# Transposing normed tiles by DMA instead of by TensorE in a macaron decoder layer

## The chip, the cores and the metric

The kernel runs on the 8 cores of one Trainium2 chip. Every core does the same program on its own prompt of 2048 tokens and its own 16 running sequences of 8 new tokens (128 tokens); nothing is exchanged between cores. The metric is the device time in microseconds of the slowest core.

## The reference

One layer: a half feed-forward, a token mixer, a second half feed-forward, and a last norm. A norm stands before each of the three parts.

```
def rmsnorm(x, g):
    inv = rsqrt(mean(x * x, axis=-1) + EPS)
    return x * inv * g

x = x + 0.5 * (silu(h @ w_gate) * (h @ w_up)) @ w_down      # h = rmsnorm(x, norm_ffn1)
B, C, u, p = split(rmsnorm(x, norm_mix) @ w_in)
y_conv = B * dwconv3_causal(C * u)
y_pool = (trailing means over 2/4/8/16 of p, minus p) @ pool_w * pool_scale
x = x + concat(y_conv, y_pool) @ w_out
x = x + 0.5 * SwiGLU_2(rmsnorm(x, norm_ffn2))
y = rmsnorm(x, norm_final)
```

D_MODEL is 1024, D_FF 2816. The states of the convolution and of the pooling are outputs too. Weights and activations come in float32; the matmuls run in bfloat16.

## The kernel before

**Data.** The 2176 tokens of a core are 17 tiles of 128. `xres` holds all of them in SBUF in float32, tokens on partitions. `hT` holds the normed tokens in bfloat16 with the features on partitions (8 blocks of 128 features), the form in which the matmuls of the gate, up and `w_in` projections take them. Between the two a tile must be transposed.

**The norm of a tile** has four steps: nA1 (ScalarE: square and row sum, line 357), nA2 (GpSimd: two tiny operations, lines 363 and 365), nA3 (VectorE: scale by the row's factor and by the weight `gbc`, into one of four bfloat16 buffers `hp`, line 370) and norm_B. norm_B is the transpose: eight TensorE transposes of 128x128 into one PSUM bank (line 387) and one ScalarE copy of the bank into `hT` (line 391). `norm_seq` lays the steps of a group of four tiles in a row: four nA1, four nA2, four nA3, four norm_B.

**The feed-forwards** (`run_ffn`) go over 6 blocks of 3 or 4 times 128 columns of D_FF, and in each over 5 groups of tokens: four of 512 tokens (four tiles) and one of 128 (tile 16). A pair (block, group) is an item. An item emits its gate and up products GU (line 454, 16 matmuls for each 128 columns; then Silu on ScalarE, line 460, and the product on VectorE, line 462), interleaved with the down products D of the item before (line 484, two for each tile, each added to `xres` on VectorE, line 491). In block 0 the norm steps of group g+1 are merged among the D of item (0, g), so the first GU of item (0, g+1) needs tiles whose norms end in item (0, g). In the last block of the first feed-forward the norms for the mixer are merged in the same way, one item later, and are read only in the mixer.

**The mixer** goes over 8 groups of 256 prompt tokens and one of 128 (lines 526, 548, 682, 704). The norms of the last five tiles for it are set into its first two groups by `LATE_SCHED`; the norms of tiles 0 to 3 for the second feed-forward are put into groups 2 to 7 by `trickle`; those of tiles 4 to 7 begin in group 8, and their norm_B stand in item (0, 0) of the second feed-forward.

**Queues.** The order on every engine is the order in which the program emits operations. Loads of weights (float32 in DRAM to bfloat16 in the six `ring` slots) are issued from GpSimd; loads of tokens, of `gbc` and the outputs are issued from SP. The loads of tokens 8 to 16 wait for the first block of down weights. The weights of block 1 are issued when the last TensorE operation of item (0, 0) is done.

Of the kernel before, what the change touches and what calls it, by code (L numbers as in the profile page):

```python
# [132 lines left out]
def build_nc():  # L133
# [216 lines left out]
    def hpbuf(k):  # L350
        return hp[:, k, :] if k < 3 else hp3[:, :]
# [22 lines left out]
    tb_cnt = [0]  # L374
    tb_banks = [[7, 6]]

    def norm_B(tt, bank=None):
        k = hp_of[tt]
        if bank is None:
            bank = tb_banks[0][tb_cnt[0] % len(tb_banks[0])]  # L380
            tb_cnt[0] += 1
        pst = ps[bank][:, :].bitcast(BF16)

        def pe_fn(e):
            ins = None
            for kc in range(KC):
                ins = e.transpose(out=pst[:, kc * 128:(kc + 1) * 128], in_=hpbuf(k)[:, kc * 128:(kc + 1) * 128],  # L387
                                  identity=idb[:, :])
            return ins
        P.op("pe", pe_fn, reads=[("hp", k), ("idb",)], writes=[("ps", bank)])  # L390
        P.op("act", lambda e: e.activation(out=hT[:, :, tt * 128:(tt + 1) * 128],  # L391
                                           in_=pst.rearrange("p (a b) -> p a b", a=KC), func=AF.Copy),
             reads=[("ps", bank)], writes=[("hT", tt)])
# [538 lines left out]
            emit()  # L932
        return []

    norm_tiles(FG[0][2])
    load_first_block(2, len(BLOCKS[0]), False)

    def after_lead1():
# [20 lines left out]
    def ffn1_post(g):  # L959
        if not state.get("gbc_mix"):  # L960
# [2 lines left out]
        return norm_seq(FG[g][2])  # L963

    late_norm = run_ffn(1, pre1, ffn1_post, ffn1_block_start, tail_fn=lambda: load_mix_units(["p", "o0"]),
                        defer_tail=True, lead=12, after_lead=after_lead1)

    def ffn2_slots(b):
        return (3, 0, 1) if b % 2 == 0 else (2, 4, 5)
# [5 lines left out]
    def mixer_phase2_setup():  # L975
# [6 lines left out]
    assert len(late_norm) == 4 * len(LT) and len(LT) == 5  # L982
    LATE_SCHED = {
        0: [(nA1, LT[0]), (nA2, LT[0]), (nA1, LT[1]), (nA2, LT[1])],
        1: [(nA1, LT[2]), (nA2, LT[2]), (nA3, LT[0])],
        2: [(nA1, LT[3]), (nA2, LT[3]), (nA3, LT[1]), (norm_B, LT[0])],
        3: [(nA3, LT[2]), (norm_B, LT[1])],
        4: [(nA1, LT[4]), (nA2, LT[4]), (nA3, LT[3]), (norm_B, LT[2])],
        5: [(nA3, LT[4]), (norm_B, LT[3])],
        6: [(norm_B, LT[4])],  # L990
    }
    trickle = {}
    for t in range(4):
        trickle.setdefault((t + 2, 1), []).append(lambda t=t: nA1(t))
        trickle.setdefault((t + 2, 2), []).append(lambda t=t: nA2(t))
        trickle.setdefault((t + 3, 1), []).append(lambda t=t: nA3(t))
        trickle.setdefault((t + 4, 1), []).append(lambda t=t: norm_B(t))
    tb_banks[0] = [5, 6]
    for g in range(9):
        if g == 2:  # L1000
# [70 lines left out]
    for g in range(1, len(FG)):  # L1071
        pre2[(0, g - 1)] = norm_seq(FG[g][2])
    so_stage, so_fin = sample_state_out_seq()
    pre2[(0, 0)] = so_stage + [lambda t=t, i=i: norm_B(t, bank=4 + i % 2) for i, t in enumerate(FG[1][2])] + so_fin
    run_ffn(2, pre2, ffn2_post, ffn2_block_start, post_now=True, last_order=[4, 0, 1, 2, 3])

    fin = P.op("sp", lambda e: None)
# [68 lines left out]
```

How the kernel before makes its waits and increments, by code:

```python
    def emit_engine(self, e, eng):  # L121
        waited = {}
        for o in self.byeng[e]:
            ws = [(d.sem, d.val) for d in o.waits] + o.extra_waits
            for (s, v) in ws:
                if waited.get(s, 0) < v:
                    eng.wait_ge(s, v)
                    waited[s] = v
            ins = o.fn(eng)
            if o.sig and ins is not None:
                ins.then_inc(o.sem, 16 if o.dma else 1)
```

## Time and profile before

| | |
|---|---|
| median of 3 runs | 1284.82 us (1284.4 to 1289.32) |
| span of the profiled execution, slowest core (core 7) | 1284.4 us, the same as the fastest of the three times |
| spans of the 8 cores | 1266.5 to 1284.4 us |
| TensorE (PE) busy | 1198.6 us, 93% |
| VectorE (DVE) busy | 596.5 us, 46% |
| ScalarE (ACT) busy | 322.9 us, 25% |
| GpSimd (POOL) busy | 162.6 us, 13% |
| packets of the DMA queues | 21.4% of 16 engines for GpSimd's queue, 5.0% for SP's |

The page follows one execution on its slowest core. "Idle before" is the time in which an engine did nothing ahead of an instruction, with what released it; idle time of an engine that is not the bottleneck costs nothing.

### The profile page before, as it was taken

Reading aid. Unit: us, or ns where it says so; the run is one execution under the profiler, and the core shown is the slowest. Engines: PE = TensorE matmul, PEld = TensorE weight load, DVE = VectorE, ACT = ScalarE, POOL = GpSimd, SP = SyncE. Lnnn points to the kernel's source line nnn. Section 1 sums busy time; section 2 is a strip of 40 time slices with the busy share of each in tenths; the row PEclk is TensorE's granted clock in tenths of the full one; section 3 lists DMA queues with packets and bytes.
Section 4 is the critical chain, followed back from the end, with each engine's and each line's share of the span. In section 5 each row is a group of like instructions: output and inputs, shape, how many; then the busy total and the mean of one; then the engine's idle time right before and its main releaser. Section 6 shows DMA issues by size and latency. Waiting matters only on the chain.

```text
span 1284.4 us, 19776 instructions; the slowest of 8 cores (1266.5 to 1284.4 us)
## 1 busy us (share of the span) xinstructions
PE 1198.6 (93%) x6916; PEld 626.8 (49%) x6916; DVE 596.5 (46%) x933; ACT 322.9 (25%) x714; POOL 162.6 (13%) x283
## 2 busy tenths in 40 slices
PE   3869999999999999979999979999999999999994
PEld 1434544445445444567676744454454454444541
DVE  2345434334334354665555552643443343444567
ACT  3342111111111112664354444421111111111133
POOL 4210000000000001233324240000000000000022
PEclk9889999999999999999999999999999999999998
DMA  9870600600403114050000057016014031040024
GB/s 174 152 185 6 98 13 1 99 1 4 71 1 47 29 29 71 1 102 18 1 2 2 1 86 131 1 17 98 2 26 74 1 51 25 1 74 1 11 105 164
DMA packets 51281, 63.37 MB, mean 49 GB/s; under 512 B 12479, under 2 KB 39103, under 8 KB 51184
## 3 DMA queue, kind: packets, MB, share of 16 engines
q0 software_dynamic: 42768, 41.03, 21.4%
q1 hardware_dynamic: 8416, 21.08, 5.0%
q8 instruction: 57, 0.93, 0.3%
q14 instruction: 40, 0.33, 0.1%
HBM read 93.63 MB, written 9.50 MB: 80 GB/s over the span
## 4 chain that ended last, share of the span: by engine, by line
PE 83%; DMA 6%; DVE 4%; ACT 3%; issue 3%; POOL 1%; SPq 0%; DVEq 0%; ACTq 0%; POOLq 0%
PE ps L454 48%; PE ps L484 24%; PE ps L526 6%; DMA ring<-ffn_up 3%; PE ps L548 2%; DMA xres<-xp 2%; PE ps L704 2%; ACT hT L391 1%; PE ps L387 1%; DMA ring<-ffn_down 1%; DVE tbuf L660 1%; ACT hp L357 1%; DVE xres L491 1%; DVE hp L370 0%; DVE hT L844 0%
## 5 line engine op out<-in xcount | busy, mean ns | idle before, releaser
L454 PE MATMUL ps<-hT,ring 128*128 128x512 bf16 (+1 forms) x3520 | 685.7, 349 | 11.4 <-ACT hT L391 7.8
L454 PEld LDWEIGHTS ps<-hT,ring 128*128 128x128 bf16 x3520 | 319.2, 98 | 355.8 <-issue 20.0
L484 PE MATMUL ps<-ring,scr 128*128 128x512 bf16 x1496 | 359.4, 380 | 15.6 <-DVE xres L491 15.6
L462 DVE TENSOR_TENSOR scr<-scr,ps 128x512 bf16<-128x512 f32 (+1 forms) x220 | 133.5, 607 | 506.9 <-PE ps L454 443.2
L460 ACT ACTIVATE scr<-ps 128x512 f32<-128x512 f32 (+1 forms) x220 | 117.0, 533 | 755.5 <-PE ps L454 749.1
L491 DVE SCALAR_TENSOR_TENSOR xres<-ps,xres 128x512 f32<-128x512 f32 x408 | 275.9, 689 | 52.3 <-PE ps L484 45.7
L484 PEld LDWEIGHTS ps<-ring,scr 128*128 128x128 bf16 x1496 | 143.4, 98 | 180.4 <-issue 23.0
L526 PE MATMUL ps<-hT,ring 128*128 128x256 bf16 (+1 forms) x864 | 95.9, 269 | 4.4 <-ACT scr L649 3.1
L526 PEld LDWEIGHTS ps<-hT,ring 128*128 128x128 bf16 x864 | 80.4, 99 | 15.9 <-issue 5.9
L357 ACT ACTIVATE hp<-xres 128x1024 bf16<-128x1024 f32 x68 | 71.1, 1050 | 43.0 <-DMA xres<-xp 34.0
L370 DVE SCALAR_TENSOR_TENSOR hp<-xres,stt,gbc 128x1024 bf16<-128x1024 f32 x51 | 64.7, 1285 | 24.2 <-POOL stt L365 23.2
L252 POOL DMA_DIRECT2D ring<-ffn_gate x11 | 10.0, 911 | 500.9 <-PE ps L454 491.4
L704 PE MATMUL ps<-ring,scr 128*128 128x512 bf16 x272 | 61.3, 379 | 5.9 <-DVE xres L711 4.9
L387 PE MATMUL ps<-idb,hp 128*128 128x128 bf16 x408 | 33.7, 231 | 33.4 <-DVE hp L370 29.1
L363 POOL TENSOR_TENSOR stt<-stt,deps_t 128x1 f32<-128x1 f32 x68 | 19.6, 289 | 342.5 <-ACT hp L357 311.4
L391 ACT ACTIVATE hT<-ps 128x1024 bf16<-128x1024 bf16 x51 | 51.2, 1021 | 31.7 <-PE ps L387 31.3
L387 PEld LDWEIGHTS ps<-idb,hp 128*128 128x128 bf16 x408 | 27.5, 103 | 45.8 <-issue 40.6
L704 PEld LDWEIGHTS ps<-ring,scr 128*128 128x128 bf16 x272 | 26.0, 98 | 37.8 <-issue 9.3
L365 POOL TENSOR_TENSOR stt<-stt,nhalf 128x1 f32<-128x1 f32 x68 | 41.0, 603 | 10.1 <-POOL stt L363 0.4
L711 DVE TENSOR_TENSOR xres<-ps,xres 128x512 f32<-128x512 f32 x34 | 22.7, 685 | 22.1 <-PE ps L704 22.1
L548 PE MATMUL ps<-hT,ring 128*128 128x256 bf16 (+1 forms) x288 | 31.2, 267 | 0.8 <-ACT scr L687 0.8
L548 PEld LDWEIGHTS ps<-hT,ring 128*128 128x128 bf16 x288 | 26.8, 98 | 3.9 <-issue 1.0
(86 smaller groups left out, 335.5 us busy)
## 6 DMA issues: line engine op xcount, KB each, us to landing
xres<-xp SPq DMA_DIRECT2D x16, 512.0 KB, 13.0
ring<-ffn_down POOLq DMA_DIRECT2D x8, 1024.0 KB, 10.0
ring<-ffn_gate POOLq DMA_DIRECT2D x7, 1024.0 KB, 10.0
ring<-ffn_up POOLq DMA_DIRECT2D x7, 1024.0 KB, 14.3
ring<-w_in POOLq DMA_DIRECT2D x4, 1024.0 KB, 10.4
yp<-hT SPq DMA_DIRECT2D x8, 512.0 KB, 2.7
ring<-ffn_gate POOLq DMA_DIRECT2D x4, 768.0 KB, 8.4
ring<-ffn_up POOLq DMA_DIRECT2D x4, 768.0 KB, 11.6
```

The source lines that it names most:

```text
L357: P.op("act", lambda e: e.activation(out=hpbuf(k), in_=xres[:, tt, :], func=AF.Square, accum_out=stat(k, 0)), reads=[("x", tt, 0), ("x", t ...
L370: P.op("dve", lambda e: e.scalar_tensor_tensor(out=hpbuf(k), in0=xres[:, tt, :], scalar=stat(k, 2), in1=gbc[:, :], op0=ALU.mult, op1=ALU.m ...
L387: ins = e.transpose(out=pst[:, kc * 128:(kc + 1) * 128], in_=hpbuf(k)[:, kc * 128:(kc + 1) * 128], identity=idb[:, :])
L391: P.op("act", lambda e: e.activation(out=hT[:, :, tt * 128:(tt + 1) * 128], in_=pst.rearrange("p (a b) -> p a b", a=KC), func=AF.Copy), re ...
L454: ins = e.matmul(ps[bank][:, 0:N], lhsT=ring_gu(slot)[:, kc, jj * 128:(jj + 1) * 128], rhs=hT[:, kc, tok0:tok0 + N], start=(kc == 0), stop ...
L460: P.op("act", lambda e: e.activation(out=sg[:, sk, 0:N], in_=ps[gb][:, 0:N], func=AF.Silu), reads=[("ps", gb)], writes=[("sg", sk)])
L462: P.op("dve", lambda e: e.tensor_tensor(out=aT[:, buf, jj, 0:N], in0=sg[:, sk, 0:N], in1=ps[ub][:, 0:N], op=ALU.mult), reads=[("sg", sk), ...
L484: ins = e.matmul(ps[db][:, 0:512], lhsT=aT[:, buf, jj, ti * 128:(ti + 1) * 128], rhs=ring_dn(ds)[:, jj, dh * 512:(dh + 1) * 512], start=(j ...
L491: P.op("dve", lambda e: e.scalar_tensor_tensor(out=xs_, in0=ps[db][:, 0:512], scalar=0.5, in1=xs_, op0=ALU.mult, op1=ALU.add), reads=[("ps ...
L526: ins = e.matmul(psh(h)[:, 0:N], lhsT=ring_gu(slot)[:, kc, col * 128:(col + 1) * 128], rhs=hT[:, kc, tok0:tok0 + N], start=(kc == 0), stop ...
L548: ins = e.matmul(ps[bank][:, (gi % 2) * 256:(gi % 2) * 256 + N], lhsT=ring_gu(slot)[:, kc, gi * 128:(gi + 1) * 128], rhs=hT[:, kc, G["tok0 ...
L704: ins = e.matmul(ps[ob][:, 0:512], lhsT=mixT[:, mb, c, ti * 128:(ti + 1) * 128], rhs=ring_dn(slot)[:, c % 4, dh * 512:(dh + 1) * 512], sta ...
```

## The change

norm_B becomes one DMA transpose, issued from SP: it reads the tile in `hp` and writes its place in `hT`. The program gives it blocks of 16 rows by 128 columns, so a tile is 64 of them. Only the first four tiles of the first feed-forward still go through TensorE, by `norm_B_pe`. 47 of 51 tiles change. The transposes that were set apart from their nA3 in the mixer follow it more closely, those of tiles 4 to 7 for the second feed-forward now stand in the mixer's last group, and all four of tiles 4 to 7 of the first feed-forward are emitted ahead of the first GU (`lead` 16 and not 12).

```diff
-    def norm_B(tt, bank=None):
+    def norm_B(tt):
         k = hp_of[tt]
-        if bank is None:
-            bank = tb_banks[0][tb_cnt[0] % len(tb_banks[0])]
-            tb_cnt[0] += 1
+        P.op("sp", lambda e: e.dma_start_transpose(out=hT[:, :, tt * 128:(tt + 1) * 128], in_=hpbuf(k)),
+             reads=[("hp", k)], writes=[("hT", tt)], dma=True)
+
+    def norm_B_pe(tt):
+        k = hp_of[tt]
+        bank = tb_banks[0][tb_cnt[0] % len(tb_banks[0])]
+        tb_cnt[0] += 1
         pst = ps[bank][:, :].bitcast(BF16)
...
-    norm_tiles(FG[0][2])
+    for c_ in norm_seq(FG[0][2], last=norm_B_pe):
+        c_()
...
-                        defer_tail=True, lead=12, after_lead=after_lead1)
+                        defer_tail=True, lead=16, after_lead=after_lead1)
...
-        3: [(nA3, LT[2]), (norm_B, LT[1])],
+        3: [(nA3, LT[2]), (norm_B, LT[2])],
...
-        trickle.setdefault((t + 4, 1), []).append(lambda t=t: norm_B(t))
+        trickle.setdefault((t + 3, 2), []).append(lambda t=t: norm_B(t))
...
             for t_ in FG[1][2]:
                 nA3(t_)
+                norm_B(t_)
             mix_wout(8)
...
-    pre2[(0, 0)] = so_stage + [lambda t=t, i=i: norm_B(t, bank=4 + i % 2) for i, t in enumerate(FG[1][2])] + so_fin
+    pre2[(0, 0)] = so_stage + so_fin
```

On SP's queue, at the start of the kernel, the difference reads as follows (`xres<-xp` are token loads, `xs` is tile 16, `gbc<-norm_mix` the mixer's norm weight):

```order
 L337 DMA sp_in<-spl 120x2x512
+L379 DMA_TRANSPOSE hT<-hp 128x8x128 x4
 L305 DMA xres<-xp 128x1024 x8
 L305 DMA xres<-xs 128x1024
+L379 DMA_TRANSPOSE hT<-hp 128x8x128 x9
 L309 DMA gbc<-norm_mix 128x1024
```

The transposes of tiles 4 to 7 now stand ahead of the loads of tokens 8 to 16, those of tiles 8 to 16 behind them.

On TensorE, the start of the kernel before: the transposes of tiles 0 to 3 (x32), then the GU of item (0, 0) with the transposes of tiles 4 to 7 between them, and the first GU of item (0, 1) at the end.

```order
L387 MATMUL ps<-idb,hp 128x128 x32
L454 MATMUL ps<-hT,ring 128x512 x16
L387 MATMUL ps<-idb,hp 128x128 x8
L454 MATMUL ps<-hT,ring 128x512 x16
L387 MATMUL ps<-idb,hp 128x128 x8
L454 MATMUL ps<-hT,ring 128x512 x16
L387 MATMUL ps<-idb,hp 128x128 x8
L454 MATMUL ps<-hT,ring 128x512 x16
L387 MATMUL ps<-idb,hp 128x128 x8
L454 MATMUL ps<-hT,ring 128x512 x16
```

And after the change, where line 391 is the transpose, 458 GU and 488 D:

```order
L391 MATMUL ps<-idb,hp 128x128 x32
L458 MATMUL ps<-hT,ring 128x512 x80
L488 MATMUL ps<-ring,scr 128x512 x8
L458 MATMUL ps<-hT,ring 128x512 x16
L488 MATMUL ps<-ring,scr 128x512 x8
```

The 80 matmuls are the four GU of item (0, 0) and the first of item (0, 1) in a row; nothing of tiles 4 to 7 stands between them any more.

On TensorE, the end of item (0, 2) of the first feed-forward before, with the transposes of tiles 12 to 15 among the last D, up to the first GU of item (0, 3):

```order
L454 MATMUL ps<-hT,ring 128x512 x16
L484 MATMUL ps<-ring,scr 128x512 x8
L454 MATMUL ps<-hT,ring 128x512 x16
L387 MATMUL ps<-idb,hp 128x128 x8
L484 MATMUL ps<-ring,scr 128x512 x4
L387 MATMUL ps<-idb,hp 128x128 x16
L484 MATMUL ps<-ring,scr 128x512 x4
L387 MATMUL ps<-idb,hp 128x128 x8
L454 MATMUL ps<-hT,ring 128x512 x16
```

The same place after the change:

```order
L458 MATMUL ps<-hT,ring 128x512 x16
L488 MATMUL ps<-ring,scr 128x512 x8
L458 MATMUL ps<-hT,ring 128x512 x16
L488 MATMUL ps<-ring,scr 128x512 x8
L458 MATMUL ps<-hT,ring 128x512 x16
```

The four transposes are gone; D and GU stand in the order they had.

## Rows read from the trace of the kernel before

**Rows 1.** Page, chain that ended last: shares of the span by engine.

```profile
PE 83%; DMA 6%; DVE 4%; ACT 3%; issue 3%; POOL 1%; SPq 0%; DVEq 0%; ACTq 0%; POOLq 0%
```

**Rows 2.** Page, groups of instructions: busy us, mean ns | idle before.

```profile
L387 PE MATMUL ps<-idb,hp 128*128 128x128 bf16 x408 | 33.7, 231 | 33.4 <-DVE hp L370 29.1
...
L391 ACT ACTIVATE hT<-ps 128x1024 bf16<-128x1024 bf16 x51 | 51.2, 1021 | 31.7 <-PE ps L387 31.3
```

**Rows 3.** Timeline, mixer, group 8's start: start us, us, instruction.

```profile
733.05 0.61 PE L387 MATMUL ps<-idb,hp 128*128 128x128 bf16 x8
733.50 5.49 PE L526 MATMUL ps<-hT,ring 128*128 128x256 bf16 x48
```

**Rows 4.** Timeline, end of item (0, 2), first feed-forward.

```profile
105.42 0.61 PE L387 MATMUL ps<-idb,hp 128*128 128x128 bf16 x8
...
106.04 1.27 DVE L370 SCALAR_TENSOR_TENSOR hp<-xres,stt,gbc 128x1024 bf16<-128x1024 f32 x1
...
107.43 3.01 ACT L391 ACTIVATE hT<-ps 128x1024 bf16<-128x1024 bf16 x3 [0.29 <-PE ps L387]
...
107.85 1.03 PE L484 MATMUL ps<-ring,scr 128*128 128x512 bf16 x4
...
110.58 3.61 PE L454 MATMUL ps<-hT,ring 128*128 128x512 bf16 x16 [1.26 <-ACT hT L391]
```

**Rows 5.** Timeline, end of item (0, 3): tile 16.

```profile
125.34 1.28 DVE L370 SCALAR_TENSOR_TENSOR hp<-xres,stt,gbc 128x1024 bf16<-128x1024 f32 x1
...
131.75 1.06 PE L454 MATMUL ps<-hT,ring 128*128 128x128 bf16 x16
```

**Rows 6.** DMA issues of the whole run: KB each, median us to landing.

```profile
yp<-hT SPq DMA_DIRECT2D x8, 512.0 KB, 2.7
...
ring<-ffn_gate POOLq DMA_DIRECT2D x4, 256.0 KB, 15.0
...
xres<-xs SPq DMA_DIRECT2D x1, 512.0 KB, 25.8
...
hp<-sc SPq DMA_DIRECT2D x1, 64.0 KB, 1.8
```

**Rows 7.** DMA queues in 0 to 38 us: packets, MB, share of 16 engines.

```profile
q0 software_dynamic: 8839, 2.23, 65.6%
```

**Rows 8.** Timeline, first feed-forward, items (0, 1) and (0, 2).

```profile
57.72 0.70 SPq L305 DMA_DIRECT2D xres<-xs  x1
...
74.23 3.57 PE L484 MATMUL ps<-ring,scr 128*128 128x512 bf16 x8 [8.40 <-DVE xres L491]
...
86.43 3.61 PE L454 MATMUL ps<-hT,ring 128*128 128x512 bf16 x16 [1.27 <-ACT hT L391]
```

**Rows 9.** Timeline, mixer, group 1.

```profile
576.52 1.01 PE L387 MATMUL ps<-idb,hp 128*128 128x128 bf16 x8 [3.10 <-DVE hp L370]
...
583.13 0.38 PE L682 MATMUL ps<-scr,poolw 128*128 128x256 bf16 x2 [1.45 <-DVE scr L611]
584.35 0.61 PE L387 MATMUL ps<-idb,hp 128*128 128x128 bf16 x8 [0.84 <-DVE hp L370]
```

**Rows 10.** Windows: stretch, PE, PEld, DVE, ACT, POOL busy, PEclk, DMA share, GB/s.

```profile
577.00:580.00 3.00, 3.00 (x20) 2.29 (x18) 2.18 (x5) 0.40 (x2) 2.48 (x4) 0.54 0.00 0
```

**Rows 11.** Timeline, start of the second feed-forward, TensorE.

```profile
769.61 2.31 PE L454 MATMUL ps<-hT,ring 128*128 128x512 bf16 x8 [3.54 <-DMA ring<-ffn_up]
771.71 1.06 PE L387 MATMUL ps<-idb,hp 128*128 128x128 bf16 x8
772.57 4.50 PE L454 MATMUL ps<-hT,ring 128*128 128x512 bf16 x16
776.90 1.06 PE L387 MATMUL ps<-idb,hp 128*128 128x128 bf16 x16
...
779.22 3.62 PE L454 MATMUL ps<-hT,ring 128*128 128x512 bf16 x16
```

More of the change, by code:

```diff
@@ L984, in build_nc @@
         0: [(nA1, LT[0]), (nA2, LT[0]), (nA1, LT[1]), (nA2, LT[1])],
-        1: [(nA1, LT[2]), (nA2, LT[2]), (nA3, LT[0])],
-        2: [(nA1, LT[3]), (nA2, LT[3]), (nA3, LT[1]), (norm_B, LT[0])],
-        3: [(nA3, LT[2]), (norm_B, LT[1])],
-        4: [(nA1, LT[4]), (nA2, LT[4]), (nA3, LT[3]), (norm_B, LT[2])],
-        5: [(nA3, LT[4]), (norm_B, LT[3])],
-        6: [(norm_B, LT[4])],
+        1: [(nA1, LT[2]), (nA2, LT[2]), (nA3, LT[0]), (norm_B, LT[0])],
+        2: [(nA1, LT[3]), (nA2, LT[3]), (nA3, LT[1]), (norm_B, LT[1])],
+        3: [(nA3, LT[2]), (norm_B, LT[2])],
+        4: [(nA1, LT[4]), (nA2, LT[4]), (nA3, LT[3]), (norm_B, LT[3])],
+        5: [(nA3, LT[4]), (norm_B, LT[4])],
     }
```

## Prediction, made before the changed kernel was run

> **What bounds the kernel now.** I read the page's chain of waits first: TensorE is 83% of it, DMA 6% [rows 1], so time that leaves TensorE's queue is time saved wherever nothing else comes last just behind it. Then the page's groups: the transposes are 408 matmuls, 33.7 us busy, and behind each tile ScalarE copies for about 1.0 us [rows 2]. ScalarE is busy for a quarter of the span, so its 47 copies are worth little by themselves. Third, the timeline around each kind of place where a tile is transposed. There are three kinds, and the forecast is the sum over them.
>
> Quiet places, where the transposed tile is read much later: 21 tiles (12 at the end of the first feed-forward, 5 in mixer groups 0 and 1, 4 of the trickle). Tight places, where the next GU waits for the tile: tiles 12 to 15 in the first feed-forward, 8 to 11 and 12 to 15 in the second, and twice tile 16. Places where the DMA engines are full: tiles 4 to 11 of the first feed-forward and 4 to 7 of the second. Together 21 + 14 + 12 = 47.
>
> **What a tile costs TensorE.** In steady work the next matmul starts 0.45 us after the first transpose (733.05 to 733.50) [rows 3]; the 0.61 us of the row overlaps it. 47 tiles would be 21 us, 1.6%, if all were on the path and the transfers hidden.
>
> **What the DMA transpose costs** no row shows; two numbers matter. L is the time from the end of nA3 to a landed tile, e the time for which one transpose keeps all 16 engines. Below: SP's own transfers take 1.8 us for 64 KB and 2.7 us for 512 KB [rows 6], 0.9 us for 448 KB more; 256 KB would give L = 2.2 and e = 0.5. Above: the tile in pieces of 256 bytes is 1024 packets. The first weight loads are such pieces (256 KB each, 15 us to landing among others [rows 6]); in 0 to 38 us that queue has 8839 packets at 65.6% of 16 engines [rows 7], which is 0.656 x 16 x 38 / 8839 = 45 ns of one engine each, so e = 1024 x 45 ns / 16 = 2.9 us and L = 1.8 + 2.9 = 4.7. I take e = 0.9, L = 2.5: nearer the transfers of the same queue, since the upper rows are software-made, cast float32 and shared the engines with token loads.
>
> The Trainium skill ("DMA: Bandwidth & Descriptors", Latency and other measured facts) puts DMA transposes at 261 GB/s for a strided and 350 to 400 GB/s for a contiguous case; 256 KB is then an estimated 0.7 to 1.0 us. No row of this case shows it; the sum by it would be mine.
>
> **Quiet places.** 21 x 0.45 = 9.4 us. More is possible: before two late tiles TensorE waits 3.10 and 0.84 us for nA3 [rows 9]. I count neither, because the pooling matmul a few us later waits for VectorE itself (583.13, 1.45 us) [rows 9] and would simply wait longer. Ends: 5 us, if VectorE comes last for the nine tiles on either side of the mixer's start, and 13 us with those waits. Taken: -9.4. hp buffers are freed by a landing instead of by TensorE, and the next nA1 on them is 10 us or more away.
>
> **Tight groups of four.** The last nA3 ends at 106.04 + 1.27 = 107.31; the GU starts at 110.58, 3.27 us later, behind transpose and copy [rows 4]. After the change TensorE has only the two D left after 105.42, 8 matmuls, about 1.7 us [rows 4], and is free at 107.15. It then waits for 107.31 + L whatever it saved. With L = 2.5 that is 0.75 us earlier than before. But the wait is now 2.7 us long. After a wait of 3.10 us TensorE's granted clock was 0.54 for 3 us, near its level of 1.2 GHz [rows 9, 10], a loss of (1 - 0.54) x 3 = 1.4 us; after 1.26 us the 16 matmuls at 110.58 took the normal 3.61 [rows 4]. 2.7 lies between: half the price, 0.7. Net 0 for each of three groups. Ends: -1.05 each (L = 2.2, full clock) and, with e = 2.9, the four transposes queue: nA3 deliver at least 1.27 apart, so the last lands near 107.3 + 1.8 + 2.9 + (3 x 2.9 - 3.8) = 116.9, +6.3, with the clock +7.7 each.
>
> **Tile 16, twice.** nA3 ends at 126.62, the GU starts at 131.75 [rows 5]: 5 us, enough for any L above. -0.45 each, -0.9.
>
> **Start of the kernel.** TensorE no longer stands still for tile 4 in the middle of item (0, 0) and reaches item (0, 1) some 3 us earlier. That is lost again: ScalarE, in order, stands at nA1 for tokens 8 to 11, TensorE waits 8.40 us until 74.23 [rows 8], and those loads hang on the down weights. The new transposes of tiles 4 to 7 take some of that load's bandwidth: +0.5. The next point is worse. The loads of tokens 8 to 16 are all in SP's queue by 58 us, the last lands at 57.7 + 25.8 = 83.5 [rows 6, 8]. Transposes 8 to 11 are issued before that and stand behind them. They end at 84.0 + 4 x 0.9 + 0.6 of landing = 88.2 with the engines alone and 91.8 when weights take every second packet; I take 90. The GU of item (0, 2) started at 86.43 [rows 8]: +3.6. TensorE then has waited for 7 us, and restarts slowly: after the 8.40 us wait 8 D took 3.57 us where 4 take 1.03 [rows 4, 8], so another +1.9 with what follows. Together +5.5; ends 0 (e = 0.5) and +14 (e = 2.9).
>
> **Start of the second feed-forward.** Removed: four tiles, 0.86 us (771.71 to 772.57) and 2.3 us (776.90 to 779.22) [rows 11], 3.2 us at a reduced clock. Added: the transposes now run just when TensorE waits 3.54 us for the up weights [rows 11], on full engines, and push that landing by 4e = 3.6. Net +0.4; ends -1.2 and +8.4.
>
> **Sum.** -9.4 + 0 - 0.9 + 5.5 + 0.4 = -4.4 us on the profiled 1284.4 (which is also the fastest of the three times; the median is 0.4 above): 1280.
>
> **Rivals.**
> 1. Transposes as cheap as copies (e = 0.5, L = 2.2). For it: SP's plain transfers [rows 6]. -11 quiet, -3.2 tight, -0.9, 0 at the start, -1.2: -16, about 1268. Chance 0.23.
> 2. Transposes that queue. The engines need 2 us or more for one, so in each tight group the fourth lands after TensorE has long been free. Price at e = 2.9: +14 + 3 x 7.7 + 8.4 - 10.3 = +35, about 1320; at e = 2 about half, 1300. It decides from e of about 1.2 us, where the start costs 7, the groups 1 each, the second start 1.6, against 10.3 gained. For it: small packets cost 45 ns each [rows 7]. Against: nothing else loads the engines in the tight groups. Chance 0.27.
> 3. The eight 128x128 blocks of a tile run one after another, each with the 1.8 us of a small transfer [rows 6]: 14 us a tile, each tight group some 50 us late, the start too, above 1450. Against it: the program moves a tile by one instruction. Chance 0.02. The skill ("VectorE: DVE Perf Modes", The three transpose paths) lists 1309 ns for a 128x128 transpose by DMA and 390 for TensorE, an estimate of 10.5 us a tile if blocks do not overlap.
> 4. Nothing changes because VectorE and DMA are last wherever TensorE gave way: quiet places give 5 us, the start takes them: 1284. Chance 0.08.
>
> **How the numbers follow.** My own case, 1274 to 1288, has 0.40. A change below 0.5% (6.4 us) can't be told from none. Faster: all of rival 1 and 0.13 of my case, 0.36. Slower: 0.27 + 0.02 and little of mine, 0.30. Same: 0.34. The range, 1266 to 1304, holds my case, rival 4, nearly all of rival 1 and the nearer half of rival 2; my case alone would be 1272 to 1288.
>
> **What would show it.** Time to landing of the transposes in quiet stretches: 2.5 us in my case; 4 or more says rival 2. The first GU of item (0, 3) should follow the last nA3 by about 2.5 us after a wait of near 3 us; the clock behind it decides the half price. The first GU of item (0, 2) should come later than 86.4 although item (0, 1) began earlier. The mixer should be shorter by about 4 us. I am wrong if the start costs nothing (then faster) or if the wait ahead of the tight GUs is above 5 us (then slower).

## The result

| | before | changed |
|---|---|---|
| time, median | 1285.55 us | 1332.4 us |
| the runs that the ratio rests on | | 1324.11, 1325.07, 1339.73 us |
| ratio | | 1.0338, interval 1.0264 to 1.0412 |
| span of the profiled execution | 1284.4 us | 1323.5 us (core 4; 1308.1 to 1323.5) |
| mean granted clock of TensorE, by core | 0.986 to 0.992 | 0.961 to 0.969 |

The forecast was 1280 us, between 1266 and 1304. The changed kernel is 3.4% slower, some 43 us: the forecast was wrong in sign, and the range did not hold the time. The fourth run of the changed kernel, 1341.35 us with one half of the chip slower than the other, counts in the median and not in the ratio.

The page of the changed kernel, section 3 (queues), section 4 (chain) and one group of section 5:

```profile
q1 hardware_dynamic: 58048, 33.41, 10.8%
...
PE 79%; DMA 7%; DVE 5%; issue 3%; SPq 3%; ACT 2%; POOL 1%; DVEq 0%; ACTq 0%; POOLq 0%
PE ps L458 46%; PE ps L488 23%; PE ps L530 5%; DMA hT<-hp 5%; SPq L379 3%; PE ps L708 2%; PE ps L552 2%; DVE hp L370 1%; DMA ring<-ffn_up 1%; DVE tbuf L664 1%; DMA xres<-xp 1%; DVE xres L495 1%; ACT hp L357 0%; DVE hT L848 0%; DVE scr L664 0%
...
L458 PE MATMUL ps<-hT,ring 128*128 128x512 bf16 (+1 forms) x3520 | 697.2, 353 | 61.5 <-DMA hT<-hp 46.2
```

Against [rows 1], TensorE fell from 83% to 79% of the chain, and SP's queue came in with 3%. The transposes' landings (`DMA hT<-hp`) hold 5% of the span, and SP's line 379, the transpose instruction itself, 3%. Together 8% of the chain is a thing that was not there.

TensorE's waits in the changed kernel: total us, times, longest us.

```profile
PE ps L458 <- DMA hT<-hp: 46.2, 6, 13.6
...
PE ps L530 <- ACT scr L653: 15.9, 6, 13.0
```

Six waits hold 46.2 us, and a seventh, 13.0 us in the mixer, is put down to ScalarE. The timeline shows all seven. First the first feed-forward, which answers to [rows 4, 8] (core 4, start us, us, instruction, idle before):

```profile
58.70 6.08 PE L458 MATMUL ps<-hT,ring 128*128 128x512 bf16 x16 [9.82 <-DMA hT<-hp]
...
95.64 6.37 PE L458 MATMUL ps<-hT,ring 128*128 128x512 bf16 x16 [13.60 <-DMA hT<-hp]
...
118.02 1.28 DVE L370 SCALAR_TENSOR_TENSOR hp<-xres,stt,gbc 128x1024 bf16<-128x1024 f32 x1
122.65 3.57 PE L458 MATMUL ps<-hT,ring 128*128 128x512 bf16 x8 [3.37 <-DMA hT<-hp]
```

The waits of 9.82 and 13.60 us are those ahead of items (0, 1) and (0, 2), where the transposes run beside weight and token loads. The third, 3.37 us, is a tight group on free DMA engines: the last nA3 ends at 119.30 and the GU starts 3.35 us later, where it was 3.27 us with transpose and copy. And behind a wait the 16 matmuls take up to 6.5 us (6.52 behind the third; the row above is cut at its window's end) where they took 3.61 [rows 4].

The mixer's entry, the same view:

```profile
558.07 24.38 SPq L379 DMA_TRANSPOSE hT<-hp  x4
...
566.73 4.72 PE L530 MATMUL ps<-hT,ring 128*128 128x256 bf16 x32
571.90 1.06 ACT L357 ACTIVATE hp<-xres 128x1024 bf16<-128x1024 f32 x1 [14.77 <-DMA hT<-hp]
...
582.81 1.06 ACT L357 ACTIVATE hp<-xres 128x1024 bf16<-128x1024 f32 x1 [9.76 <-DMA hT<-hp]
...
584.47 0.80 PE L530 MATMUL ps<-hT,ring 128*128 128x256 bf16 x3 [13.02 <-ACT scr L653]
```

Here is the wait that names ScalarE. ScalarE is not busy: its nA1 of the next late tiles writes an `hp` buffer, and waits 14.77 and 9.76 us for the transposes that still read those buffers. Behind nA1, in ScalarE's order, stands the evacuation (L653) that TensorE needs. One must follow a releaser that is not busy to its own.

The start of the second feed-forward, answering to [rows 11]:

```profile
787.10 29.47 SPq L379 DMA_TRANSPOSE hT<-hp  x4
...
797.37 7.03 PE L458 MATMUL ps<-hT,ring 128*128 128x512 bf16 x24 [4.90 <-DMA ring<-ffn_up]
...
824.57 5.44 PE L458 MATMUL ps<-hT,ring 128*128 128x512 bf16 x16 [11.96 <-DMA hT<-hp]
```

From the start of the first to the end of the last, four transposes take 29.47 us, and SP stands in them for nearly all of it (1.3 to 10.8 us each). The remaining two waits (3.45 us at 850.73, 3.97 us at 875.58) are tight groups like the first.

What a transpose takes, by stretch, is in the view of line 379: duration on SP min/median/max ns, and time to landing. The stretches are 525 to 534 us (late norms of the last block), 556 to 575 (mixer's entry) and 786 to 817 (second feed-forward):

```profile
L379 SPq DMA_TRANSPOSE hT<-hp x4: 1231/1234/1248, 528.4 to 533.8; - x4
...
DMA to landing us min/median/max: 3.0/3.1/3.3
...
L379 SPq DMA_TRANSPOSE hT<-hp x3: 1254/5820/13349, 558.1 to 565.9; - x3
...
DMA to landing us min/median/max: 13.8/17.7/22.9
...
L379 SPq DMA_TRANSPOSE hT<-hp x4: 1338/8424/10786, 787.1 to 808.0; - x4
...
DMA to landing us min/median/max: 16.0/18.6/23.1
```

One instruction, one size: 3.1 us on free engines and 18 us beside loads. The second view shows three of the mixer's four; the fourth was issued later.

Start times on core 4 of both profiled executions give the account, in us:

| | before | changed | later by |
|---|---|---|---|
| GU of (0, 3), first feed-forward | 104.10 | 122.65 | 18.6 |
| first matmul of the mixer | 547.08 | 566.73 | 19.7 |
| `w_out` of the mixer's first group | 584.4 | 620.14 | 35.7 |
| GU of (0, 0), second feed-forward | 757.70 | 790.57 | 32.9 |
| GU of (0, 2), second feed-forward | 806.43 | 850.73 | 44.3 |
| span | 1277.8 | 1323.5 | 45.7 |

Three steps, +19, +16 and +11 us. Between them the lag changes little: +1.1, -2.8 and +1.4 us. So the stretch with the twelve quiet tiles at the end of the first feed-forward shows no gain on this core. The mixer, which was to be 4 us shorter, took 223.8 us and not 210.6.

### The profile page after: what moved, and what is told of

It reads as the page before. It is cut to its first block, busy times and chain, and to the rows that moved or that the text cites. A ratio compares the mean times of both kernels' runs of the same rounds, so it can differ in the third digit from the quotient of the medians.

```text
span 1323.5 us, 19140 instructions; the slowest of 8 cores (1308.1 to 1323.5 us)
## 1 busy us (share of the span) xinstructions
PE 1191.1 (90%) x6540; PEld 609.4 (46%) x6540; DVE 597.2 (45%) x933; ACT 277.6 (21%) x667; POOL 163.5 (12%) x283
## 3 DMA queue, kind: packets, MB, share of 16 engines
q1 hardware_dynamic: 58048, 33.41, 10.8%
## 4 chain that ended last, share of the span: by engine, by line
PE 79%; DMA 7%; DVE 5%; issue 3%; SPq 3%; ACT 2%; POOL 1%; DVEq 0%; ACTq 0%; POOLq 0%
PE ps L458 46%; PE ps L488 23%; PE ps L530 5%; DMA hT<-hp 5%; SPq L379 3%; PE ps L708 2%; PE ps L552 2%; DVE hp L370 1%; DMA ring<-ffn_up 1%; DVE tbuf L664 1%; DMA xres<-xp 1%; DVE xres L495 1%; ACT hp L357 0%; DVE hT L848 0%; DVE scr L664 0%
## 5 line engine op out<-in xcount | busy, mean ns | idle before, releaser
L458 PE MATMUL ps<-hT,ring 128*128 128x512 bf16 (+1 forms) x3520 | 697.2, 353 | 61.5 <-DMA hT<-hp 46.2
L458 PEld LDWEIGHTS ps<-hT,ring 128*128 128x128 bf16 x3520 | 321.8, 99 | 418.7 <-issue 88.6
L530 PE MATMUL ps<-hT,ring 128*128 128x256 bf16 (+1 forms) x864 | 100.5, 276 | 19.2 <-ACT scr L653 15.9
L530 PEld LDWEIGHTS ps<-hT,ring 128*128 128x128 bf16 x864 | 83.0, 101 | 34.8 <-issue 21.8
L365 POOL TENSOR_TENSOR stt<-stt,nhalf 128x1 f32<-128x1 f32 x68 | 44.5, 655 | 10.0 <-POOL stt L363 0.4
L552 PE MATMUL ps<-hT,ring 128*128 128x256 bf16 (+1 forms) x288 | 31.2, 267 | 0.7 <-ACT scr L691 0.7
L655 DVE TENSOR_TENSOR vext<-scr,ps 128x256 f32<-128x256 f32 x32 | 13.4, 420 | 35.1 <-ACT scr L653 25.4
L552 PEld LDWEIGHTS ps<-hT,ring 128*128 128x128 bf16 x288 | 26.9, 98 | 4.1 <-issue 1.1
L664 DVE SCALAR_TENSOR_TENSOR tbuf<-vext,cw,tbuf 128x256 f32<-128x256 f32 x32 | 18.6, 582 | 17.9 <-ACT vhalo L672 16.2
L664 DVE SCALAR_TENSOR_TENSOR scr<-vext,cw,scr 128x256 f32<-128x256 f32 x32 | 17.4, 543 | 14.9 <-ACT vhalo L672 12.4
## 6 DMA issues: line engine op xcount, KB each, us to landing
ring<-ffn_down POOLq DMA_DIRECT2D x8, 1024.0 KB, 11.4
```

The costliest lines, as they stand in the source:

```text
L365: P.op("pool", lambda e: e.tensor_tensor(out=stat(k, 2), in0=stat(k, 1), in1=nhalf[:, :], op=ALU.pow), reads=[("st", k), ("nhalf",)], writ ...
L458: ins = e.matmul(ps[bank][:, 0:N], lhsT=ring_gu(slot)[:, kc, jj * 128:(jj + 1) * 128], rhs=hT[:, kc, tok0:tok0 + N], start=(kc == 0), stop ...
L530: ins = e.matmul(psh(h)[:, 0:N], lhsT=ring_gu(slot)[:, kc, col * 128:(col + 1) * 128], rhs=hT[:, kc, tok0:tok0 + N], start=(kc == 0), stop ...
L552: ins = e.matmul(ps[bank][:, (gi % 2) * 256:(gi % 2) * 256 + N], lhsT=ring_gu(slot)[:, kc, gi * 128:(gi + 1) * 128], rhs=hT[:, kc, G["tok0 ...
L664: P.op("dve", lambda e, ve=ve, i=i, k=k, tb=tb: e.scalar_tensor_tensor(out=v3(tb[:, 0:N]), in0=ve[:, :, k:k + T], scalar=cw[:, i * 3 + k:i ...
```

## The experiments

**The transpose by itself.** A kernel without the model: four transfers of 256 KB each from SP, as transposes, as plain copies with 2 KB rows, and as plain copies in pieces of 256 bytes; alone, and beside three 1 MB weight loads from GpSimd.

```diff
+dma_start_transpose(out=hT[:, :, k*128:(k+1)*128], in_=hpbuf(k))                        # L258 alone, L262 beside loads
+dma_start(out=hT[:, k, 0:1024], in_=hpbuf(k))                                           # L270, L274: 2 KB rows
+dma_start(out=hT[:, :, k*128:(k+1)*128], in_=hpbuf(k).rearrange("p (a b) -> p a b", a=8)) # L278, L283: 256 B
```

> A kernel with the model left out: it only moves a tile of 256 KB four times in each of eight stages, from SP. Theory 'sharing' (a transpose is 1024 packets of 256 bytes, cheap alone, and beside weight loads each of its packets waits for a large weight packet): four transposes alone land 3.3 us after issue each and hold the engines about 1 to 1.6 us each; beside three 1 MB weight loads they take 8 to 12 us each; plain copies cut into 256-byte pieces beside the same loads are about as slow (over 6 us each), plain copies in 2 KB pieces much faster (2 to 5 us). Rival 'the transpose itself': the 256-byte copies beside weights stay below 5 us and only transposes take 8 us or more. Rival 'queue order': transposes alone behind five token loads land late by the loads' time (5 to 8 us), and beside weights, with nothing ahead of them in SP's queue, they stay near 3.3 us.

The view of each line; first alone (transposes L258, 2 KB copies L270), then beside the loads (2 KB copies L274, 256 B copies L283, transposes L262):

```profile
L258 SPq DMA_TRANSPOSE hT<-hp x4: 1330/1338/1348, 6.6 to 10.8; - x4
...
DMA to landing us min/median/max: 3.1/3.3/3.4
...
L270 SPq DMA_DIRECT2D hT<-hp x4: 560/590/610, 14.1 to 16.0; - x4
...
DMA to landing us min/median/max: 2.4/2.5/2.5
...
L274 SPq DMA_DIRECT2D hT<-hp x4: 527/650/806, 55.8 to 57.9; - x4
...
DMA to landing us min/median/max: 8.6/9.9/10.8
...
L283 SPq DMA_DIRECT2D hT<-hp x4: 632/4036/8737, 85.0 to 95.7; - x4
...
DMA to landing us min/median/max: 15.0/18.1/23.1
...
L262 SPq DMA_TRANSPOSE hT<-hp x4: 1478/5409/8880, 116.3 to 133.3; - x4
...
DMA to landing us min/median/max: 7.6/13.7/19.4
```

Alone a transpose needs 0.8 us more than a plain copy with 2 KB rows, and the copy in 256 B pieces (L278) more than either, 3.8 us. Beside loads all three are slow: 9.9 us for the large rows, where 2 to 5 had been expected, 13.7 for the transposes, 18.1 for the small copies. So the transposing itself is not the price: it is to share the engines with the loads, and more so in small pieces. With nothing ahead of them in SP's queue the transposes were slow all the same, so the order of the queue is not needed for it. In the changed kernel SP's queue has (58048 - 8416) / 47 = 1056 packets for each transpose, where the prediction had 1024. The Trainium skill ("DMA: Bandwidth & Descriptors", Queues, rings and completion order) says that a DMA engine takes turns between its queues by the packet, and that one packet may hold several descriptors. If a turn of small pieces moves fewer bytes than a turn of the weights, the small copies must fall behind; L283 against L274, the same bytes at nearly twice the time, fits that, but what one turn holds no run here shows. Why the transposes do somewhat better than the copies of the same piece stays open. Transposes issued behind five token loads, without weights, landed in 3.4 to 9.0 us.

**The order on SP's queue.** In the changed kernel the loads of tiles 12 to 16 are issued behind the transposes of tiles 8 to 11:

```diff
-        for tt in range(8, NT):
+        for tt in range(8, 12):
             load_x(tt)
...
+    pre1[(0, 1)] = pre1[(0, 1)] + [lambda tt=tt: load_x(tt) for tt in range(12, NT)]
```

> The changed kernel, but SP issues the token loads of tiles 12 to 16 only after the transposes of tiles 8 to 11. In the changed kernel the first GU of item (0, 2) waits 13.6 us for those transposes and starts at 95.6 us. Rival 'queue order' (the transposes stand behind the token loads in SP's queue, the step of the prediction): the wait falls to 3 us or less, start at 86 or earlier, total 8 to 10 us shorter. Theory 'sharing': the weights of block 1 are still in flight, the wait stays at 8 us or more, and the total changes by less than 5 us.

Timeline of core 6, and the landings of tiles 8 to 11:

```profile
86.58 3.15 PE L458 MATMUL ps<-hT,ring 128*128 128x512 bf16 x7 [3.34 <-DMA hT<-hp]
...
DMA to landing us min/median/max: 3.1/6.0/8.0
```

The wait ahead of item (0, 2) fell to 3.34 us (13.60 on core 4 of the changed kernel, 13.24 on its core 6); those ahead of items (0, 1) and (0, 3) stayed, 11.51 and 3.55 us. So these transposes did stand behind the token loads, as the prediction had it. Still beside the weights of block 1, they landed within 3.1 to 8.0 us. The two runs, 1319.21 and 1329.83 us, give no price: the 8 to 10 us that were expected are neither shown nor excluded.

**The weights of block 1 held back** until behind the first GU of item (0, 2) in the changed kernel (the expectation says its end; the first was issued at 89.53 us):

```diff
-            load_after[0] = (P.byeng["pe"][-1],)
-            load_ffn_block(1, 1)
-            load_after[0] = ()
             return
...
+    pre1[(0, 2)] = [load_block1] + pre1[(0, 2)]
```

> The changed kernel, but the three weight loads of block 1 are issued at the end of item (0, 2) and not after item (0, 0), so none is in flight beside the transposes of tiles 8 to 11, and they are beside those of tiles 12 to 15 or 16 instead. 'Sharing': the 13.6 us wait before item (0, 2) falls below 4 us. The waits before items (0, 3) (3.4 us in the changed kernel) or (0, 4) grow where the weights now meet the transposes. Total 8 to 15 us shorter if they meet nothing tight, else about unchanged. 'Queue order': the wait falls too, but the later waits do not grow.

Timeline of core 5: items (0, 2) and (0, 3).

```profile
84.56 4.36 PE L458 MATMUL ps<-hT,ring 128*128 128x512 bf16 x16 [2.46 <-DMA hT<-hp]
...
119.34 3.15 PE L458 MATMUL ps<-hT,ring 128*128 128x512 bf16 x7 [9.41 <-DMA hT<-hp]
```

1339.47 us, ratio 1.0415 (1.0361 to 1.0470). The wait of item (0, 2) went, and a wait of 9.41 us appeared at item (0, 3), whose transposes now meet the weights: landings 3.0/7.8/11.3 us, where they had been 3.0/3.2/3.2. This moves the collision and shows it: the same four transposes, slow only because weights are on the way. It also limits the reading of the experiment before. Here all nine token loads still stood ahead of the transposes of tiles 8 to 11, and these landed in 3.1 to 3.5 us, since the tokens themselves came early: tile 16's in 12.8 and 12.6 us on cores 0 and 2, where the changed kernel has 22.9 and 22.0. Either edit alone takes the wait away, so it needs both: token loads ahead in the queue, and weights that hold these loads up. The whole time is not a clean price, since two cores of the profiled run (4 and 5) had a lower clock, 0.943 and 0.946 against 0.960 to 0.966.

**Which tiles pay, on the kernel before.** norm_B goes by DMA for a chosen set of tiles in each part, else through TensorE:

```diff
+        if tt in BY_DMA[phase[0]]:
+            k = hp_of[tt]
+            P.op("sp", lambda e: e.dma_start_transpose(out=hT[:, :, tt * 128:(tt + 1) * 128], in_=hpbuf(k)),
+                 reads=[("hp", k)], writes=[("hT", tt)], dma=True)
+            return
```

All 21 quiet tiles of the prediction:

> The kernel before, with DMA transposes only for the 21 quiet tiles: all 17 norms of the mixer, at the places of the changed kernel, and tiles 0 to 3 of the second feed-forward. 26 other tiles stay on TensorE. Theory 'sharing': the group of tiles 8 to 11 meets the loads of w_in and w_out, its hp buffers come free late, ScalarE stands at nA1 and TensorE waits about 13 us at the mixer's entry as in the changed kernel; total 5 to 12 us slower than before (1291 to 1297). Rival 'only the tight places cost': 9 us faster, 1276.

17 of them, without the mixer's tiles 8 to 11:

> As the one with the 21 quiet tiles by DMA, but tiles 8 to 11 of the mixer's norm stay on TensorE, so no transpose runs beside the loads of w_in and w_out: 17 tiles by DMA. 'Sharing': no wait of over 4 us at the mixer's entry, total 5 to 8 us faster than before (17 x 0.45 = 7.7), 1277 to 1280. Rival 'landings of hp are late anyway': the wait stays near 10 us.

The 14 tight tiles alone (three groups, twice tile 16):

> The kernel before, with DMA transposes only at the tight places that no weight load meets: tiles 12 to 16 of the first feed-forward, 8 to 16 of the second, 14 tiles. With 3.3 us to landing each group of four gains nothing and restarts at the low clock: +1.5 to +2.5 us each for three groups, -0.45 for each tile 16; total 3 to 7 us slower, 1288 to 1292. Rival 'cheap as copies': 2 to 4 us faster.

17 quiet and 14 tight, so all but the sixteen tiles beside loads:

> The kernel before with DMA for the 17 quiet tiles of one run and the 14 tight ones of another; the 16 tiles that meet weight loads stay on TensorE. If the places add up, the sum of the two: 0 to 4 us faster than before (1281 to 1285), and 38 us or more faster than the changed kernel, which then is the cost of the 16 tiles alone.

| | tiles | ratio | interval |
|---|---|---|---|
| all quiet | 21 | 1.0051 | 1.0033 to 1.0069 |
| quiet without the mixer's 8 to 11 | 17 | 0.9960 | 0.9946 to 0.9973 |
| tight | 14 | 1.0043 | 1.0029 to 1.0057 |
| 17 quiet and 14 tight | 31 | none | shortest 1291.43 and 1300.02 us |

The seven runs of the last scatter up to 1429.53 us (median 1368.34), so it has no ratio. Its two shortest are 33 and 24 us below the changed kernel's shortest, 1324.11, but not in the 1281 to 1285 us that were expected. "All quiet" against "17" is the mixer's tiles 8 to 11 alone: 0.9% or 11.7 us for four tiles that I had counted at -1.8. Timeline of "all quiet", core 0:

```profile
545.03 39.09 SPq L382 DMA_TRANSPOSE hT<-hp  x7
...
557.21 1.06 ACT L357 ACTIVATE hp<-xres 128x1024 bf16<-128x1024 f32 x1 [13.15 <-DMA hT<-hp]
...
568.83 4.08 PE L536 MATMUL ps<-hT,ring 128*128 128x256 bf16 x24 [11.10 <-ACT scr L659]
```

The same chain as in the changed kernel, and in the version with 17 tiles the longest such wait is 1.2 us. The two versions differ in these four tiles alone. The tight tiles lose: 0.43% is 5.5 us, with two single tiles at perhaps -0.9 some 2 us for each group of four. Timeline of "tight", core 3:

```profile
113.91 2.72 PE L464 MATMUL ps<-hT,ring 128*128 128x512 bf16 x6 [3.60 <-DMA hT<-hp]
```

Six matmuls take 2.72 us there, 0.45 each, and 16 took 3.61 at full clock, 0.23 each.

**One group undone at a time, on the changed kernel.** The mixer's tiles 8 to 11 through TensorE:

```diff
+        if phase[0] == "mix" and tt in (8, 9, 10, 11):
+            norm_B_pe(tt)
+            return
```

> The changed kernel with one thing undone: the four transposes of tiles 8 to 11 for the mixer go through TensorE again, all others stay on DMA. Theory (these four stand beside the loads of w_in and w_out and land 14 to 23 us late, so the hp buffers for tiles 12 and on come free late, ScalarE's nA1 stands in its queue, and TensorE waits 13 us in the mixer's second group): 13 to 16 us less than the changed kernel, about 1310 us, ratio to the kernel before 1.020 to 1.023, and no wait of TensorE at the mixer's entry above 2 us. Rival (the mixer is late because of the transposes of tiles 12 to 16 there, or because of a lower clock): less than 5 us gained, ratio 1.03 or more.

The second feed-forward's tiles 4 to 7, at their old places:

```diff
                 nA3(t_)
-                norm_B(t_)
...
-    pre2[(0, 0)] = so_stage + so_fin
+    pre2[(0, 0)] = so_stage + [lambda t=t, i=i: norm_B_pe(t, bank=4 + i % 2) for i, t in enumerate(FG[1][2])] + so_fin
```

> The changed kernel with one thing undone: tiles 4 to 7 of the second feed-forward go through TensorE again, at the places they had before, in item (0, 0). Theory (beside the first weights of the second feed-forward they land 16 to 23 us late, and the wait of 12 us ahead of item (0, 1) is theirs): 9 to 12 us less than the changed kernel, ratio 1.024 to 1.027, and that wait gone but for the 1.3 us behind ScalarE's copy. Rival (the up weights of that block come late by themselves, because other transfers keep the engines): a wait of 8 us or more stays, with the up weights as its releaser, ratio 1.03 or more.

The first feed-forward's tiles 4 to 7:

```diff
+        if phase[0] == "f1" and tt in (4, 5, 6, 7):
+            norm_B_pe(tt)
+            return
...
-                        defer_tail=True, lead=16, after_lead=after_lead1)
+                        defer_tail=True, lead=12, after_lead=after_lead1)
```

> The changed kernel with one thing undone: tiles 4 to 7 of the first feed-forward go through TensorE again, at the places they had before, between the GU of item (0, 0). All others stay on DMA, tiles 8 to 11 behind the token loads on SP's queue. Theory (the start is set by the later of two waits, and the transposes of tiles 8 to 11, which stand behind the token loads, come last whatever item (0, 1) does): item (0, 1) begins some 7 us earlier, but TensorE waits for the landing of tiles 8 to 11 for some 20 us instead of 13.6, and the kernel gains less than 3 us, ratio 1.031 or more. Rival (the two waits add up): 7 to 10 us gained, ratio 1.026 to 1.028.

And its tiles 4 to 11, the same with (4, ..., 11):

> The changed kernel with tiles 4 to 11 of the first feed-forward on TensorE again, at the places they had before. The other 39 stay on DMA. Theory (in the account of start times the first three items lose 18.6 us, and all of it is these eight transposes): 17 to 21 us less than the changed kernel, ratio 1.017 to 1.020, and the three undone groups (this one, the mixer's tiles 8 to 11 with 15 us, the second feed-forward's tiles 4 to 7 with 8 us) together explain the 43 us that the change costs. Rival (the start loses for another reason as well, since transposes 12 to 16 meet the weights of block 1, or the token loads come later): less than 12 us gained, ratio 1.024 or more, and a wait of TensorE for DMA landings of hT of 8 us or more stays ahead of item (0, 3).

| undone | ratio to before | interval | gain on the changed kernel |
|---|---|---|---|
| mixer, 8 to 11 | 1.0221 | 1.0185 to 1.0257 | 15.1 us |
| second feed-forward, 4 to 7 | 1.0272 | 1.0238 to 1.0307 | 8.5 us |
| first feed-forward, 4 to 7 | 1.0307 | 1.0281 to 1.0332 | 4.0 us |
| first feed-forward, 4 to 11 | 1.0209 | 1.0184 to 1.0234 | 16.6 us |

The gain is the difference to 1.0338 times 1288 us. 15.1 + 8.5 + 16.6 = 40.2 of the 43.5 us. Each gain carries the uncertainty of the changed kernel's own ratio (0.0074), so no single one is better known than to some 10 us, and the sum, in which that ratio stands three times, less well. Three comparisons do without it: the mixer's four cost 11.7 us on the kernel before; tiles 8 to 11 of the first feed-forward, undone on top of 4 to 7, gave 12.6 us (1.0307 to 1.0209, one chip); and with the other 31 tiles on DMA the kernel came to 24 to 33 us below the changed one. The account of start times, from one core, has 16, 11 and 19. So the sixteen tiles beside loads are most of the loss; what each group has of it is known only roughly. The groups for the second feed-forward and for the start came out just short of the 9 to 12 and 17 to 21 us expected. With the second feed-forward's group undone the wait of 12 us was gone, and that for the up weights stood at 3.7 us (3.5 before), so late up weights are not the cause.

Tiles 4 to 7 alone can't be told from no gain. The timelines say why they would give little; first "4 to 7 undone" (core 3):

```profile
53.22 3.61 PE L463 MATMUL ps<-hT,ring 128*128 128x512 bf16 x16 [1.27 <-ACT hT L400]
...
93.77 5.19 PE L463 MATMUL ps<-hT,ring 128*128 128x512 bf16 x16 [18.28 <-DMA hT<-hp]
```

and "4 to 11 undone" (core 4):

```profile
86.63 3.40 PE L463 MATMUL ps<-hT,ring 128*128 128x512 bf16 x15 [1.48 <-ACT hT L400]
...
110.69 5.30 PE L463 MATMUL ps<-hT,ring 128*128 128x512 bf16 x15 [3.40 <-DMA hT<-hp]
```

Item (0, 1) starts early (60.62 on core 3 of the changed kernel), then item (0, 2) waits 18.28 us for tiles 8 to 11 and starts at 93.77, only 2 us before the changed kernel's 95.90. The later of the two waits covers the earlier. It does so only while the earlier is short. The wait for tiles 4 to 7 was 4.4 to 11.4 us on the cores of the changed kernel, but 18.7 to 22.2 us on two cores each in the runs "mixer undone" and "second feed-forward undone", their slowest among them, and there item (0, 2) began at 101.9 to 103.8 us. So the gains of these two groups may be larger than the table has them. With both groups undone item (0, 2) starts at 86.63, as in [rows 8].

**A version that hides the landing.** The 17 quiet tiles and tile 16 twice, by DMA:

```diff
+    BY_DMA = {'f1': [16], 'mix': [0, ..., 7, 12, ..., 16], 'f2': [0, 1, 2, 3, 16]}
```

> The kernel before with 17 quiet tiles by DMA (as in the version that was 0.4% faster) and tile 16 of both feed-forwards too. Theory (a transposed tile costs only where less than 3.3 us lie between its nA3 and its reader, or where weight loads run): tile 16 has 5 us, so no wait behind it and 0.45 us less each, ratio 0.995 to 0.996, the waits of TensorE for DMA landings of hT under 0.5 us in all. Rival (every transposed tile that is read soon costs a wait, since a single landing in the model is later than the quiet 3.3 us): a wait of 2 us or more ahead of the GU of tile 16, ratio 0.998 or more.

Then the norms of the three tight groups merged among the first three D of their item, with five D behind them; the groups still on TensorE:

```diff
+            elif (f, b, g) in EARLY:      # (1,0,2), (2,0,1), (2,0,2)
+                interleave(gu, merge(extra, dd[:3]) + dd[3:])
```

> c_singles, with the norms of the three tight groups (tiles 12 to 15 of the first feed-forward, 8 to 11 and 12 to 15 of the second) merged among the first three down products of their item, so that five down products (20 matmuls, 4.3 us) stand behind the last transpose; the transposes of these groups stay on TensorE. Theory: only the wait of 1.26 us for ScalarE's copy goes, three times: -3.8 us against c_singles. Rival (VectorE, which does nA3, the product behind Silu and the addition to xres, comes last when norms are closer together): no gain, TensorE waits for VectorE among the five down products instead.

And the three groups by DMA as well (31 tiles; the expectation's 33 is a miscount):

> The same early norms, and the three tight groups by DMA as well: 33 tiles in all, every one except the sixteen beside the loads and the first two groups. Theory: the last landing is 3.3 us behind nA3 and is covered by the 20 matmuls of down products, 4.3 us, so no wait, and 12 more tiles leave TensorE at 0.45 us: -5 us against c_early_pe, ratio to the kernel before 0.987 to 0.990. Rival 1 (VectorE comes last): same as c_early_pe. Rival 2 (transposes queue in a group of four, SP being held 1.2 us each): a wait of 1 us or more ahead of the first GU of the three groups, and a slow restart, ratio 0.993 or more.

| | median | ratio | interval |
|---|---|---|---|
| single tiles too | 1284.72 us | 0.9958 | 0.9944 to 0.9973 |
| early norms, TensorE | 1283.02 us | 0.9949 | 0.9934 to 0.9964 |
| early norms, DMA | 1275.72 us | 0.9888 | 0.9871 to 0.9905 |

The single tiles add nothing that can be told from the 0.9960 without them. The last version is 1.1% or 14.4 us faster than the kernel before, measured on one chip with it, and by the two ratios 4.4% faster than the changed kernel. Against the same order on TensorE it gained 7.9 us, where 5 had been expected. It has no wait for a transpose at all. Its timeline, item (0, 2), core 1, and the landings of all its transposes:

```profile
102.29 1.28 DVE L370 SCALAR_TENSOR_TENSOR hp<-xres,stt,gbc 128x1024 bf16<-128x1024 f32 x1
103.80 4.97 PE L494 MATMUL ps<-ring,scr 128*128 128x512 bf16 x20
...
108.61 3.62 PE L464 MATMUL ps<-hT,ring 128*128 128x512 bf16 x16
...
DMA to landing us min/median/max: 3.0/3.1/7.5
```

The last nA3 ends at 103.57, the landing some 3.3 us later lies under 20 matmuls of D, and the GU at 108.61 comes without a wait and at full clock. The same order of norms on TensorE gave 1.1 us, which can't be told from nothing, and not the 3.8 expected: three of the six waits of GU for the copy went (7.8 us in all fell to 4.3), but the transposes themselves now wait for a bank (2.1 us rose to 4.6). The waits of TensorE with early norms on TensorE:

```profile
PE ps L397 <- ACT hT L401: 4.6, 5, 1.3
...
PE ps L464 <- ACT hT L401: 4.3, 3, 1.5
```

## Why the prediction was wrong

**The bound** was read rightly: TensorE is 83% of the chain, and of the time taken off its queue about two thirds was saved where nothing came last behind it (0.3 of 0.45 us a tile).

**The step that failed** is the list of places, and one sentence under "Quiet places": "hp buffers are freed by a landing instead of by TensorE, and the next nA1 on them is 10 us or more away." The four transposes at the mixer's entry landed in 14 to 23 us, not 2.5. Ten microseconds were no margin, and a DMA that no reader waited for stopped TensorE through the buffer it read. I had counted these tiles among the quiet ones at -1.8 us; they cost 12 us (on the kernel before) to 15 (on the changed one). The kernel before had shown that the engines are not free there. Windows of its trace, columns as in [rows 10]:

```profile
535.00:556.00 21.00, 17.53 (x165) 11.18 (x163) 15.77 (x24) 15.28 (x25) 6.12 (x14) 1.00 0.46 73
556.00:576.00 20.00, 15.99 (x156) 13.73 (x153) 12.16 (x27) 12.61 (x34) 8.09 (x14) 1.00 0.45 87
```

The DMA engines are 45% busy in the mean (the last number but one), with `w_in` and `w_out` on the way; a load of each was issued at 545 and 546 us, another of `w_out` at 554. In the changed kernel the stretch reads:

```profile
555.00:586.00 31.00, 13.55 (x77) 7.59 (x76) 10.44 (x16) 4.84 (x14) 5.25 (x11) 0.72 0.88 136
```

88%, and TensorE's clock at 0.72.

**The price beside loads** was the second error, and the same one in size. At both starts I added e = 0.9 us for each transpose to a stream of loads, as if a transpose took only its own time from full engines. In fact most land 10 to 23 us after their issue (3.3 to 14.8 at the start, 16.0 to 23.1 at the second feed-forward, core 4). Start of the kernel: +5.5 forecast (ends 0 and +14), +16.6 measured. Second feed-forward: +0.4 forecast (ends -1.2 and +8.4), +8.5 measured, at its upper end. The start had the right mechanism for tiles 8 to 11, the queue behind the token loads. Tile 16's tokens landed at 82.9 us on core 4, as taken (83.5); the four transposes behind them then needed 12.7 us, beside weights that were on the way until 91.7, where the sum had 6.5: landed by 95.6 us, not 90. And the sum left its own +0.5 for tiles 4 to 7 out of the 5.5 (3.6 + 1.9) without a word; they began item (0, 1) 7 us late (58.70 against 51.65 on core 4).

**L and e in quiet places.** L was 3.1 to 3.3 us, taken 2.5, ends 2.2 and 4.7. e follows from the queue's share: (10.8% of 1323.5 - 5.0% of 1284.4) / 47 = 1.7 us of all 16 engines for each, taken 0.9. That mean holds the packets beside loads too. In 528 to 538 us of the changed kernel nothing but four transposes is on the engines (packets, MB, share):

```profile
q1 hardware_dynamic: 4224, 1.05, 54.5%
```

That is 1056 packets and 1.4 us for each, and e on free engines. The 0.7 to 1.0 us that the prediction estimated from the Trainium skill ("DMA: Bandwidth & Descriptors", Latency and other measured facts) is not reached. Either value is above the 1.2 from which I let rival 2 decide, but its mechanism, transposes that queue up in a tight group, was not seen: SP is held 1.23 us for each and nA3 deliver 1.27 us apart, so four just follow one another. With e = 1.4 and L = 3.3 the prediction's own terms would be about +8 at the start, +2 at the second, +2 for each tight group, and the sum about 1290 us (an estimate). So the sizes of L and e are not the missing 40 us; how late a transpose lands beside loads is.

**Quiet places** gave 5.1 us for 17 tiles (interval 3.5 to 7.0), 0.3 us each where I took 0.45. Right in kind, within the ends.

**Tight groups:** net 0 forecast, about +2 us each measured, ends -1.05 and +7.7. The wait was 3.4 to 4 us, not 2.7, and the restart can cost twice the full price of 1.4 us that the sum halved: on core 4 the 16 matmuls at 122.65 take 6.5 us in all against 3.61. Those at 875.58 take 5.30, those at 850.73 the normal 3.61.

**Together**, measured less forecast: the mixer's four 14 to 17 us, the start 11, the second start 8, the tight groups 6, the quiet tiles 3. That is 42 to 45 of the 48 us between the forecast of -4.4 and the 43.5 measured.

**The criteria set beforehand:** item (0, 2) did come after 86.4 us although (0, 1) should have begun earlier (it did not); the wait of tight groups stayed under 5 us; the start did not cost nothing. So the result is slower by none of the two named ways. The nearest rival in time, 2 at 1320, was near by the size of its terms for the two starts, not by its reason. Rival 3 is out: a tile lands in 3.1 us, not 14. Of rival 1, the cheap transpose, nothing was left at L = 3.3.

## What to carry to other kernels

A DMA in place of an engine's work must be priced by the traffic at the moment it runs: the same 256 KB landed in 3 us on free engines and in 18 beside weight loads. List the loads under each place before calling it quiet, and ask not only who reads what the DMA writes but also who waits for the buffer it reads, and what stands ahead of it on its own queue. Where the engines are free, give it its landing time in work of the waiting engine (here five down products), and leave the loaded places as they were.

## What the runs showed of the hardware

- A transpose of 128x1024 bf16 in SBUF from SP: 3.0 to 3.4 us to landing on free engines, 1056 packets and 1.4 us of all 16 engines, SP held for 1.23 us each (1.34 in the kernel without the model); 0.8 us more than a plain copy with 2 KB rows (2.4 to 2.5).
- Beside three 1 MB loads from GpSimd the same copy took 8.6 to 10.8 us, the transpose 7.6 to 19.4, a copy in 256 B pieces 15.0 to 23.1. SP itself is held: 21.32 us for four transposes, 17.58 for four small copies.
- After waits of 3.4 to 13.6 us TensorE mostly comes back at the lower of its two clocks (1.2 GHz, 0.45 us for a matmul of 512 columns, against 0.23 at 2.4). After the same wait of 3.4 us, ahead of item (0, 3), core 0 ran its 16 in 3.61 us and core 4 took 6.5. Core 4 itself does both, after 3.37 and after 3.45 us (windows as in [rows 10]; the granted clock is the last number but two):

```profile
122.70:126.20 3.50, 3.50 (x9) 1.24 (x10) 0.00 (x0) 0.00 (x0) 0.00 (x0) 0.50 0.00 0
850.80:854.00 3.20, 3.20 (x16) 1.42 (x16) 0.00 (x0) 1.24 (x2) 0.00 (x0) 1.00 0.00 0
```

What tells them apart no run here shows.
